# A decoder layer with routed experts: narrow router products, a third expert's rows by one-hot products, second buffers, and products of zeros in the routing's waits

## What is computed

```python
scores = sigmoid(t @ router_w)                    # t is x1, 1024 x 1024; router_w is 1024 x 16
sel = scores + router_bias                        # best group of 4 experts, then its best 2
top_w = top_w / sum(top_w)                        # the gates
y += gate[:, e:e+1] * ((silu(t @ w1[e]) * (t @ w3[e])) @ w2[e])      # for the tokens of expert e
out = layer_norm(ALPHA * x1 + y)
```

## Time and profile before

| | |
|---|---|
| median of 3 runs | 1025.86 us (1021.03 to 1026.15) |
| profiled execution, its own time | 1031.45 us |
| its span | 1029.6 us |
| PE busy | 933.0 us (91%) |
| DVE, ACT, POOL busy | 604.4, 475.6, 195.4 us |
| the chain that ended last | PE 85%, DVE 7%, ACT 4%, DMA 2%, issue 2% |

### The profile page before, as it was taken

One profiled execution on the slowest core, in us unless ns is written; L12 is line 12 of the kernel. 1 busy time (PEld: TensorE's weight loads), 2 busy tenths in 40 slices (PEclk: granted clock), 3 DMA queues, 4 the chain that ended last, 5 costly groups with the idle time before them and its releaser, 6 DMA issues.

```text
span 1029.6 us, 18674 instructions
## 1 busy us (share of the span) xinstructions
PE 933.0 (91%) x7178; PEld 758.9 (74%) x7178; DVE 604.4 (59%) x786; ACT 475.6 (46%) x750; POOL 195.4 (19%) x238
## 2 busy tenths in 40 slices
PE   6998999998999999979998369999999999999940
PEld 5777988995777777768887338887888888888830
DVE  2301733654564655676556817777767777777728
ACT  3311432224554654561112126666666666666614
POOL 2000000000000000010000276333434334433116
PEclk9999999998999999989998569999999999999985
DMA  9301021001010031059332168999999999999656
GB/s 255 56 21 42 21 62 41 1 1 41 22 41 21 22 72 41 1 171 398 135 123 82 27 163 257 320 316 318 311 325 323 326 309 320 314 312 321 202 139 256
DMA packets 102659, 168.10 MB, mean 163 GB/s; under 512 B 25776, under 2 KB 49328, under 8 KB 102608
## 3 DMA queue, kind: packets, MB, share of 16 engines
q1 hardware_dynamic: 88768, 145.05, 41.8%
q0 software_dynamic: 10800, 21.17, 8.6%
q10 hardware_dynamic: 3040, 1.19, 0.5%
HBM read 142.84 MB, written 24.54 MB: 163 GB/s over the span
## 4 chain that ended last, share of the span: by engine, by line
PE 85%; DVE 7%; ACT 4%; DMA 2%; issue 2%; SPq 0%; POOL 0%; POOLq 0%; ACTq 0%; DVEq 0%
PE bank L675 13%; PE bank L677 12%; PE bank L676 12%; PE pz L675 8%; PE pz L677 7%; PE pz L676 7%; PE pz L966 6%; PE pz L1006 3%; PE pz L833 3%; PE bank L846 2%; PE bank L860 2%; PE bank L955 1%; PE bank L923 1%; DMA x_row<-in_x_dram 1%; DVE cstat L1679 1%
## 5 line engine op out<-in xcount | busy, mean ns | idle before, releaser
L1544 DVE TENSOR_TENSOR el<-er,eh 128x1024 fp32r<-128x1024 f32 x192 | 225.2, 1222 | 48.7 <-ACT eh L1253 48.4
L1253 ACT ACTIVATE eh<-er 128x1024 fp32r<-128x1024 f32 x192 | 190.3, 1051 | 0.0
L1477 DVE TENSOR_TENSOR_SCAN Qs<-Qs 128x128 f32<-128x128 f32 (+7 forms) x48 | 65.0, 1354 | 78.6 <-ACT Qs L1168 78.6
L675 PE MATMUL bank<-xT_hi,w_hi 128*128 128x512 f32 x256 | 105.4, 412 | 3.3 <-DVE xT_lo L1361 3.3
L675 PE MATMUL pz<-eh,xh 128*128 128x512 f32 x256 | 103.2, 403 | 2.3 <-issue 2.2
L677 PE MATMUL pz<-eh,xl 128*128 128x512 f32 x256 | 101.0, 395 | 0.4 <-issue 0.4
L676 PE MATMUL pz<-el,xh 128*128 128x512 f32 x256 | 101.2, 395 | 0.0
L677 PE MATMUL bank<-xT_hi,w_lo 128*128 128x512 f32 x256 | 101.1, 395 | 0.0
L676 PE MATMUL bank<-xT_lo,w_hi 128*128 128x512 f32 x256 | 101.0, 394 | 0.0
L544 POOL IOTA zidl<- 112x160 uint32 x1 | 0.3, 288 | 437.7 <-ACT aT L1179 437.7
L675 PE MATMUL bank<-w_hi,xT_hi 128*128 128x384 f32 x192 | 65.9, 343 | 6.8 <-DVE w_lo L1349 5.5
(11 more groups left out here) (264 smaller groups left out, 1794.9 us busy)
## 6 DMA issues: line engine op xcount, KB each, us to landing
er<-in_w_dram SPq DMA_DIRECT2D x192, 512.0 KB
w_raw<-in_w_in_dram SPq DMA_DIRECT2D x21, 512.0 KB, 3.8
x_row<-in_x_dram SPq DMA_DIRECT2D x8, 512.0 KB, 9.7
xres<-in_x_dram SPq DMA_DIRECT2D x8, 512.0 KB, 5.4
x_scratch<-x SPq DMA_DIRECT2D x8, 512.0 KB, 2.6
sum_scratch<-x SPq DMA_DIRECT2D x8, 512.0 KB, 4.0
cx<-sum_scratch SPq DMA_DIRECT2D x8, 512.0 KB, 6.4
out_dram<-cx SPq DMA_DIRECT2D x8, 512.0 KB, 2.6
```

What stands on the lines that cost most here:

```text
L675: pe.matmul(dst, lh, rh, start=(k == k_first), stop=False)
L1253: act.activation(eh[:, p, :], er[:, p, :], ACT.Copy).then_inc(S["eh_ok"], 1)
L1477: dve.tensor_tensor_scan(Qs[:, h, 0:W][:, ::-1], Qs[:, h, 0:W][:, ::-1], Qs[:, h, 0:W][:, ::-1], 1.0, ALU.mult, ALU.min).then_inc(S["scan_ ...
L1544: dve.tensor_tensor(el[:, p, :], er[:, p, :], eh[:, p, :].bitcast(F32), ALU.subtract).then_inc(S["el_ok"], 1)
```

## The change

1. **Router products.** `rw` is padded with zeros to 32 columns (`TR`) and becomes the stationary operand; `x1T` (128 columns) streams. Slice k goes to the 32 partitions of group k % 4 of `po`. ACT copies the four groups to `lgS` (`groups_out`), and one more product with `gsum`, a 0/1 matrix made by POOL, adds them up into `pa_` (`sum_groups`, for tile i-3 after the mixing of tile i). ACT's copy stands before the `x1T` copy, and for i = 9 before four `piece_hi`.
2. **Third expert.** `DIRECT = 3`: the row numbers of expert 2 come from one-hot products too. DVE makes the one-hot rows in block 0 after `x_lo` (`slot_hits(2)`), PE the products between the `w1` and the `w3` half of block 0 (`slot_tokens(2)`), DVE the row numbers after `piece_lo` 11 (`slot_rows(2)`). POOL gathers expert 2 right after scatter(1).
3. **Products of zeros** (`spin`, 128x384, bf16): 36 before the position counts, 12 behind them, 34 behind `slot_tokens(1)` and 34 behind `slot_tokens(2)`, the latter within block 0.
4. **Own buffers** `yAs[1]`, `yBs[1]` for expert 1, whose block is written out now; the loop begins at expert 2. POOL's order behind the gathers is new: tables 0 and 1, addition 0, gates 1, tables 2 and 3, gather 3, addition 1.

```diff
+DIRECT = 3
-        rw = small("rw", [P, NK, NE])
+        rw = small("rw", [P, NK, TR])
-        yB = rt("yB", 36 * K, [P, DQ])
-        yA = rt("yA", 38 * K, [P, D])
+        yBs = [rt("yB0", 36 * K, [P, DQ]), rt("yB1", 37 * K, [P, DQ])]
+        yAs = [rt("yA0", 38 * K, [P, D]), rt("yA1", 0, [P, D])]
...
             block(NE * j, True)
-            with eng.Fori(1, NE - 1) as e:
+            block(NE * j + 1, True, 1)
+            with eng.Fori(2, NE - 1) as e:
...
-            for b in range(2):
-                pool.wait_ge(S["first_ok"], 2 * b + 2)
+            for b in range(DIRECT):
+                if b < 2:
+                    pool.wait_ge(S["first_ok"], 2 * b + 2)
                 if b:
-                    scatter(0)
+                    scatter(b - 1)
+                if b == 2:
+                    pool.wait_ge(S["first_ok"], 2 * b + 2)
+                if b:
                     pool.wait_ge(S["xtr_ps"], NXR * b)
...
-            scatter(1)
...
+            def sum_groups(c):
+                pe.wait_ge(S["lg_ev"], c + 1)
+                pe.matmul(pa_[:, c * NE:(c + 1) * NE], lgS[:, :], gsum[:, :], start=True, stop=True).then_inc(S["lg_ps"], 1)
...
+                if i >= 3:
+                    sum_groups(i - 3)
...
                     for k in range(NK):
-                        last = pe.matmul(pa_[:, c * NE:(c + 1) * NE], x1T[:, k, :], rw[:, k, :], start=(k == 0), stop=(k == NK - 1))
-                    last.then_inc(S["lg_ps"], 1)
+                        g = k % 4
+                        last = pe.matmul(po[TR * g:TR * g + TR, 0:P], rw[:, k, :], x1T[:, k, :], start=(k < 4), stop=(k >= NK - 4),
+                                         skip_group_check=True)
+                    last.then_inc(S["lgm_ps"], 1)
+            sum_groups(NT - 1)
+            def spin(n):
+                for _ in range(n):
+                    pe.matmul(pz[1][:, 512:512 + GLA_W], zb[:, 0:P], zb[:, :], start=True, stop=True, skip_group_check=True)
+            pe.wait_ge(S["x1t_ev"], NT)
+            spin(36)
...
             last.then_inc(S["pos_ps"], 1)
+            spin(12)
...
+                if b:
+                    spin(34)
...
                 rows_gu(b, 0)
+                if first_block(b):
+                    slot_tokens(2)
                 rows_gu(b, 1)
...
+            def groups_out(c):
+                act.wait_ge(S["lgm_ps"], c + 1)
+                if c >= 1:
+                    act.wait_ge(S["lg_ps"], c)
+                act.activation(lgS[:, :], po[:, 0:P], ACT.Copy).then_inc(S["lg_ev"], 1)
...
                 if not first_block(b):
-                    act.wait_ge(S["y_out"], 32 * b)
+                    if not buf:
+                        act.wait_ge(S["y_out"], 32 * b)
                     act.wait_ge(S["slot_ok"], b + 1)
```

More of the change, by code:

```diff
@@ L231, in small @@
             return t
-        rw = small("rw", [P, NK, NE])
+        rw = small("rw", [P, NK, TR])
+        lgS = small("lgS", [P, P])
+        gsum = small("gsum", [P, NE])
         rb = small("rb", [P, NE])
@@ L543, in _ @@
             pool.wait_ge(S["conv_ok"], 10)
+            pool.memset(rw[:, :, NE:], 0.0).then_inc(S["gsum_ok"], 1)
+            pool.memset(gsum[:, :], 0.0).then_inc(S["gsum_ok"], 1)
+            for g in range(4):
+                pool.wait_ge(S["gsum_ok"], 2 + g)
+                pool.affine_select(gsum[:, :], gsum[:, :], [[-1, NE]], ALU.not_equal, 1.0, base=-TR * g, channel_multiplier=1)\
+                    .then_inc(S["gsum_ok"], 1)
             pool.iota(zidl[:, :, 0], [[1, TW]], base=T, channel_multiplier=0).then_inc(S["tokc_ok"], 1)
@@ L641, in pool_pass @@
                 b0 = NE * j
[L642 to L647, removed]
-                gates(0, b0)
-                add_rows(0, b0)
-                step(3, b0 + 3)
+                load_table(0, b0)
+                load_table(1, b0 + 1)
+                quarters(0, b0, 2)
+                quarters(1, b0 + 1)
+                if not isinstance(j, int):
+                    gather(0, b0)
+                    gather(1, b0 + 1)
+                gates(0, b0)
+                if isinstance(j, int):
+                    add_rows(0, b0)
+                    gates(1, b0 + 1)
+                load_table(2, b0 + 2)
+                load_table(3, b0 + 3)
+                quarters(2, b0 + 2, 2)
+                quarters(3, b0 + 3)
+                if not isinstance(j, int):
+                    gather(2, b0 + 2)
+                    add_rows(0, b0)
+                    gates(1, b0 + 1)
+                gather(3, b0 + 3)
+                add_rows(1, b0 + 1, 1)
                 with pool.Fori(1, NE // 4) as i:
@@ L934, in _, with slot_tokens @@
             last.then_inc(S["pos_ps"], 1)
+            spin(12)
             pe.wait_ge(S["idb_ok"], 1)
-            for b in range(2):
+            def slot_tokens(b):
                 pe.wait_ge(S["oneh_ok"], b + 1)
                 for i in range(NT):
-                    pe.matmul(sids_bank[b][0], oneh[:, b, i, 0:P], idb[:, :, i], start=(i == 0), stop=(i == NT - 1), skip_group_check=True)
+                    pe.matmul(sids_bank[b % 2][0], oneh[:, b % 2, i, 0:P], idb[:, :, i], start=(i == 0), stop=(i == NT - 1),
+                              skip_group_check=True)
                 for i in range(NT):
                     for g in range(NQ):
-                        last = pe.matmul(sids_bank[b][1][g * TR:(g + 1) * TR, :], oneh[:, b, i, P:TW], idb[:, :, i],
+                        last = pe.matmul(sids_bank[b % 2][1][g * TR:(g + 1) * TR, :], oneh[:, b % 2, i, P:TW], idb[:, :, i],
                                          start=(i == 0), stop=(i == NT - 1), skip_group_check=True)
                 last.then_inc(S["sids_ps"], 1)
+                if b:
+                    spin(34)
+            for b in range(2):
+                slot_tokens(b)
             def x_transposes(b, rounds):
@@ L1314, in act_block @@
                 act.wait_ge(S["rowsA_ps"], 2 * b + 2)
-                act.activation(yA[:, 512:], pp[1][:, :], ACT.Copy, scale=1.0 if first_block(b) else slotG[:, 0:1])\
+                act.activation(yAs[buf][:, 512:], pp[1][:, :], ACT.Copy, scale=1.0 if first_block(b) else slotG[:, 0:1])\
                     .then_inc(S["yA1_ev"], 1)
@@ L1596, in _, with slot_rows @@
                                   skey[:, b, :].unsqueeze(2).to_broadcast([P, NT, TW]), ALU.is_equal).then_inc(S["oneh_ok"], 1)
-            for b in range(2):
+            def slot_rows(b):
+                bank = sids_bank[b % 2]
                 dve.wait_ge(S["sids_ps"], b + 1)
                 for c in range(2):
-                    dve.tensor_copy(sids[:, 2 * b + c:2 * b + c + 1], sids_bank[b][c][:, 0:1]).then_inc(S["sids_ok"], 1)
+                    dve.tensor_copy(sids[:, 3 * b + c:3 * b + c + 1], bank[c][:, 0:1]).then_inc(S["sids_ok"], 1)
@@ L1606, in _ @@
                                          ALU.mult, ALU.add).then_inc(S["sids_ok"], 1)
                 dve.wait_ge(S["sids_ok"], 3 * b + 3)
-                dve.tensor_scalar(firstB[:, b:b + 1], sids[:, 4 + b:5 + b], float(NQ), quad[:, 0:1], ALU.mult, ALU.add).then_inc(S["first_ok"], 1)
+                dve.tensor_scalar(firstB[:, b:b + 1], sids[:, 3 * b + 2:3 * b + 3], float(NQ), quad[:, 0:1], ALU.mult, ALU.add)\
+                    .then_inc(S["first_ok"], 1)
+            for b in range(2):
+                slot_hits(b)
@@ L1610, in _ @@
+            for b in range(2):
+                slot_rows(b)
             link(dve.tensor_reduce(rmax[:, :], rpos[:, NT, :], AX.X, ALU.max))
```

52 lines of the change are left out of this document (32 added, 20 removed).

## The result

| | before | changed |
|---|---|---|
| median | 1027.12 us (1021.03 to 1030.49, 20 runs) | 1020.34 us (1018.15 to 1023.85, 20 runs) |
| profiled execution, its span | 1031.45, 1029.6 us | 1020.39, 1018.6 us |
| PE busy | 933.0 us | 936.9 us |
| DVE, ACT, POOL busy | 604.4, 475.6, 195.4 us | 607.0, 475.9, 202.6 us |

The ratio is 0.9935 with a 95% interval of 0.992 to 0.995: faster, by 6.7 us. The two profiled executions lie further apart, by 11.06 us, against 16.4 of the forecast; 4.3 of the 11.06 is the distance of the profiled execution before (1031.45) from the median of its own kernel. Both distances need explaining, and they have different causes.

What follows compares the result with a forecast made beforehand. PE was taken to bound the mixing and the expert loop, with block 0 slowed by the low clock and an issue stretch. Terms -5.1 + 0.5 + 0.2 - 14.5 + 2.5 = -16.4 from 1031.45 gave about 1015.0 us; range 1008 to 1026.

Steps and rivals of the forecast that it cites:

- The mixing: Router products of tiles 0 to 4: 1.02 us saved each, 5.1 off the path, less 0.5 for array-mode changes.
- the end of the logits: The last tile's router products, 3.61 us at the low clock, would take 1.9; net gain 1.3 us.
- rival A: The issue stretch in block 0 stays until the scatters end: 1020.8 up to 1026 us; chance 0.23.
- The 36: Products of zeros before the position counts: 8.1 us, cost 1.5, with the clock rising after 4 us.
- Rival C: The zeros in the three waits and block 0 don't raise the clock: +19 or 1045 us; chance 0.08.
- Block 0: From its first transposes to block 1's: 22.6 us instead of 37.1, including 2 to 5 for the zeros inside.
- -14.5: Gain in us from block 0 taking 22.6 instead of 37.1, with the issue stretch dropped from the sum.
- POOL's chain: Block 2 needs addition 1 landed by about 654, POOL is there about 650 to 660: cost 2.5 us.
- The gates of expert 1: All that block 1's yB copy needs with its own buffer; expected at about 628 us.
- A wait of over 2 us: Sign: ACT waiting on yB over 2 us in blocks 1 to 3 would show rival B.
- rival B: POOL's chain holds blocks 2 and 3, giving back block 0's gain by 6 us more: 1021 us; chance 0.10.
- Rival D: Written-out code starves PE: block 0 keeps its loss, block 1 gets another 13 us: 1034 us; chance 0.04.

Runs made afterwards that it cites:

- e2: The kernel before with part 1 (router products) alone: 1020.0 us, ratio 0.9929 to the kernel before.
- e1: The changed kernel again, without an edit: 1020.48 us, ratio 0.9936 to the kernel before.
- e4: The changed kernel with every product of zeros taken out: 1019.01 us, ratio 0.9913 to the kernel before.
- e3: The kernel before with only the zeros ahead of block 0 (36, 12 and 34) added: 1026.64 us, ratio 0.9986 to the kernel before.
- e5: The kernel before, unedited, one profiled execution on a second chip: 1040.94 us.
- e6: The changed kernel without zeros, each table's spare rows in one DMA instead of four: 1028.94 us, ratio 0.9932 to the kernel before.
- e7: The changed kernel with one-DMA spare-row tables, gather 1 ahead of both scatters, zeros only ahead of block 0: 1027.58 us, ratio 0.9915 to the kernel before.
- e12: The kernel of e6 again, on a third chip: 1026.44 us, ratio 0.9934 to the kernel before.
- e8: The kernel of e7 without any zeros: 1026.37 us, ratio 0.9898 to the kernel before.
- e9: The changed kernel again, unedited, on a third chip: 1023.33 us, ratio 0.9919 to the kernel before.
- e10: The changed kernel with one yA and one yB again, on a third chip: 1034.88 us, ratio 0.9999 to the kernel before.
- e11: The kernel of e8 again, on a third chip: 1023.88 us, ratio 0.9917 to the kernel before.

## Why the prediction was right, and where it was not

**The mixing** came as worked out: 5 x 1.02 less 0.5 for the changes between the whole array and column groups is 4.6, and five tiles of 12.65 instead of 13.5 give 4.3. At the end of the logits 1.3 was forecast: from the start of the last router products to the position counts it is 8.8 us in e2 and 10.3 before, 1.5 less. The 16 rows start after one another in 0.57 us, not 0.46, so some of the drain is inside them. The Trainium skill, "TensorEngine Tiling (Array Packing)", section Key Properties, has PE drained at each switch; the trace agrees, and the price is a tenth of a microsecond a switch at most (a tile gains 0.85 of 1.02, with two switches). So part 1 was worth 5.9 by the prediction's terms and 5.8 by the rows; alone (e2) it gives 7.1 us in the median, with an interval of 5.1 to 9.6, and so the whole measured gain. By the same terms parts 2 to 4 were to bring the other 10.5 us. In the medians they bring nothing that can be told (e1 against e2). The measured time lies 5.3 us above the forecast, in a range that reached to rival A's far end; the forecast had the source of the gain wrong.

**The zeros.** The 36 took 8.61 us against 8.1, the 34 took 5.70 against 5.8, and block 0 started 1.6 us later than without them (e4), against 1.5 of cost. They did warm the clock: it was 0.51 in the microsecond from 565 and full from then on, 5.3 us after the first product of zeros, where the prediction took 4. Rival C falls. But the full clock bought nothing (e3, e4), as the end of block 0 was not PE's.

**Block 0** took 23.1 us against 22.6, and in part by luck. The 22.6 are PE's work, with 2 to 5 us of cost in them for the zeros inside. The block ended on gather 1, 0.8 us after PE was done; in e1, the same kernel, it ended 2.6 us after, and in e4, without the zeros, at the same distance from the router products: these zeros cost nothing. And the step "-14.5" took for the kernel's what was one execution's: the loss of 14.5 us is the stretch, and the stretch comes and goes without the change. It is in the profile before, in e5, e6, e7 and e12, hardly in e8, e9, e10 and block 0 of e11, and not in the changed kernel's first two profiles nor in e2, e3 and e4. Where it is missing altogether, block 0 takes 23 to 25 us with gather 1 behind scatter(0), zeros or not. I wrote that the median lies 5.6 below the profiled execution and that the difference may be part of that stretch. The gain had to be counted from the median. Whether the executions at the median of the kernel before lack the stretch is not shown, as both its profiles have it; it fits that e3, without the stretch, took 1026.94 us in its profile, and the kernel before 1027.13 in the median on that chip.

**POOL's chain** is the term that was mis-sized: 2.5 us forecast, 7.3 measured (4.4 of waiting and 2.9 of low clock behind it); it isn't a constant either, as it was 3.4 in e1, where the clock stayed full. I looked at the addition of expert 1, which was hidden, and for block 3 should have added up two tables and gather 3 behind the first addition. The gates of expert 1, forecast for about 628, were late too, as they stand on POOL behind addition 0 (ACT, changed kernel):

```profile
634.87 0.47 ACT L1375 ACTIVATE yB<-pz,slotG 128x256 f32<-128x256 f32 x1 [3.75 <-POOL slotG L625]
```

A wait of over 2 us there was the prediction's sign for rival B; PE did not wait for it.

The mis-sized term is rival B's mechanism; of its 6 us more than the forecast's 2.5, 4.8 came, and the forecast's 1015.0 plus 4.8 and the 0.5 of block 0 is 1020.3, the measured time.

**Rival A** (the stretch stays, 1020.8 to 1026) did not happen in the profile after, but its "just the mixing's 5" names the gain of the runs better than the forecast's mechanism does. **Rival D** falls: the stretch was seen in the hardware loop too (e12 at 652 to 657, block 2, last row shown of it), while e2 and e4 run a written-out block 0 without it. Its packets of code are few as well, 37 with 0.61 MB in the changed kernel:

```profile
q8 instruction: 37, 0.61, 0.3%
```

That is 16 KiB each, as the Trainium skill, "Runtime: NRT & Kernel Launch", section Instruction fetch mechanics, says. By its rule their cost is mostly hidden. The number of packets doesn't separate the two cases: the kernel before has 33 and shows the stretch, e2 has 34 and doesn't. That code loading takes no part in the stretch is not shown.

**Is there a faster version?** The changed kernel without its zeros is as fast on one chip (0.9913 against 0.9936, intervals overlapping), and simpler. Gather 1 ahead of the scatters was 0.9898 on one chip and 0.9917 beside 0.9919 for the changed kernel on another. None beats it by more than the measurement can tell.

## What to carry to other kernels

Before pricing the end of a stage by its busy engine, ask which transfer its last instruction waits for: products that keep PE warm buy nothing while a gather lands later, and what a sooner gather wins is lost again at the next link of the same chain. Set an expected gain against the median of the runs, and not against a profiled execution from their slow end, above all when the loss that you mean to remove has no releaser. A buffer whose wait costs nothing in one profile can still move the median (e10), here by a way that no profile shows, so run such a kernel a dozen times.

## What was unexpected of the hardware

In the stretch PE starts its instructions in steps. In e12 single products of 2 columns, 0.16 to 0.18 us long, start at 600.20, 600.93, 601.63, 603.06: 0.7 us apart, or twice that. In e11 and e5 the step is the same (610.79, 611.53, 612.24). It falls on full and low clock alike (in e7 1.00 from 594 to 598 and 0.50 from 600 to 606), in block 0 (before, e5, e6, e7, e12), in block 1 (e11, 606 to 612) and in the loop (e12 from 652, e11 from 669). Busy DMA engines are not its condition: in the profile before it goes on at a DMA share of 0.03 and 0.01 (608 to 610 and 610 to 612), and in e2 PE runs without a wait at shares of 1.02 to 1.11 (586 to 594). In the profile before and in e5 the last wait ended 2.2 and 2.5 us behind the end of the last scatter's issue on POOL, in e12 1.2 us behind it (608.80 and 607.6); its return at 652 lies beside gather 3 and two additions, which are indirect DMAs too. Yet kernels with the same scatters ran without it, all four on the first chip. That POOL's indirect DMAs take part is therefore a guess, and the cause stays open.

How long PE waits does not say by itself whether the clock falls. Before block 3 PE waited 3.25 us in e1, and the granted clock was 1.00 behind the wait (656.5 to 658.3); in e10 it waited 2.56 us, and the clock was 0.51 (656.3 to 658.3).
